# Two encoder layers unrolled: counting semaphores, a norm per token tile, projections one place forward

## What is computed

```python
def reference(x, norm_g, w_in, ..., w_branch, w_out):
    for l in range(DEPTH):                       # DEPTH = 2
        h = _rms(x, norm_g[l])
        p = jnp.einsum('bsd,de->bse', h, w_in[l])            # 1024 x 11808
        (a_qkv, a_a, a_b, a_z, b_qkv, b_z, c_q, c_k, c_v, c_z,
         d_q, d_k, d_v, d_i, d_f, d_o, d_z, gate_logits) = _split(p, PROJ_SIZES)
        y_a = _mixer_deltanet(...)   # conv of 5 taps, SiLU, gated delta rule in chunks of 64, both directions
        y_b = _mixer_natten(...)     # neighbourhood attention with a learned bias
        y_c = _mixer_gqa(...)        # grouped-query attention with axial rotary
        y_d = _mixer_mlstm(...)      # mLSTM in chunks of 64, both directions
        ys = jnp.stack([y_a, y_b, y_c, y_d], axis=2)
        proj = jnp.einsum('bsnw,nwd->bsnd', ys, w_branch[l])
        merged = jnp.sum(jax.nn.sigmoid(gate_logits...) * proj, axis=2)
        x = x + jnp.einsum('bsd,de->bse', merged, w_out[l])
```

## Time and profile before

| | us |
|---|---|
| time, median of 3 runs | 983.67 (981.82 to 983.68) |
| span of the profiled execution, first to last instruction | 982.1 |
| PE busy | 903.4 (92%) |
| DVE busy | 672.2 (68%) |
| ACT busy | 497.9 (51%) |
| POOL busy | 203.0 (21%) |
| all 464 splits on DVE (L1411) | 325.6 |
| all 464 splits on ACT (L1098) | 274.0 |

### The profile page before, as it was taken

The page is one execution under the profiler, slowest core; times in us unless marked ns, Lnnn a source line. Parts: engine busy times, 40 slices in busy tenths (PEclk is TensorE's granted clock), DMA queues, the critical chain, the costliest instruction groups (busy, mean ns, idle before and its releaser), DMA issues. The chain is left out here.

```text
span 982.1 us, 19657 instructions
## 1 busy us (share of the span) xinstructions
PE 903.4 (92%) x7206; PEld 750.8 (76%) x7206; DVE 672.2 (68%) x1209; ACT 497.9 (51%) x990; POOL 203.0 (21%) x216
## 2 busy tenths in 40 slices
PE   3998999999899999999859899999998989999996
PEld 3986778787787788778658787788877768887775
DVE  3888795667368587587459887765762776866763
ACT  3545644553454565555246555544543645564651
POOL 0301221435220014121021111222542200322210
PEclk9989999999999999999959999999999999999999
DMA  7643634424376145467156346434333832544762
GB/s 205 204 135 118 203 119 131 129 90 127 90 174 190 48 150 168 130 179 228 65 133 187 124 138 209 127 111 141 105 108 98 208 124 86 152 149 129 234 195 65
DMA packets 101403, 140.13 MB, mean 143 GB/s; under 512 B 31022, under 2 KB 45494, under 8 KB 101174
## 3 DMA queue, kind: packets, MB, share of 16 engines
q1 hardware_dynamic: 94118, 137.80, 47.4%
q10 hardware_dynamic: 7184, 1.02, 0.6%
HBM read 135.63 MB, written 7.27 MB: 146 GB/s over the span
## 5 line engine op out<-in xcount | busy, mean ns | idle before, releaser
L1411 DVE TENSOR_TENSOR w_low<-ring,w_high 128x512 fp32r<-128x512 f32 x464 | 325.6, 743 | 112.5 <-ACT w_high L1098 112.4
L1098 ACT ACTIVATE w_high<-ring 128x512 fp32r<-128x512 f32 x464 | 274.0, 627 | 87.2 <-PE pj L605 44.3
L603 PE MATMUL pj<-w_high,h_high 128*128 128x512 f32 x592 | 245.1, 414 | 8.7 <-DVE w_low L1411 7.9
L605 PE MATMUL pj<-w_high,h_low 128*128 128x512 f32 x592 | 234.2, 396 | 0.0
L604 PE MATMUL pj<-w_low,h_high 128*128 128x512 f32 x592 | 234.1, 395 | 0.0
L603 PEld LDWEIGHTS pj<-w_high,h_high 128*128 128x128 f32 x592 | 113.4, 191 | 36.4 <-DVE w_low L1411 8.3
L605 PEld LDWEIGHTS pj<-w_high,h_low 128*128 128x128 f32 x592 | 112.9, 191 | 24.8
L604 PEld LDWEIGHTS pj<-w_low,h_high 128*128 128x128 f32 x592 | 113.4, 192 | 22.5 <-issue 1.0
L1103 ACT ACTIVATE big<-pair 128x512 f32<-128x512 f32 (+2 forms) x136 | 60.9, 482 | 77.0 <-PE pair L780 37.1
L603 PE MATMUL mb<-w_high,h_high 128*128 128x512 f32 x112 | 44.4, 397 | 3.1 <-DVE h_low L1860 3.1
L1933 POOL TENSOR_TENSOR big<-big,tab 128x256 f32<-128x256 f32 x40 | 34.6, 881 | 48.6 <-ACT big L1255 25.0
(11 more groups left out here) (282 smaller groups left out, 1553.6 us busy)
## 6 DMA issues: line engine op xcount, KB each, us to landing
ring<-in_w_in SPq DMA_DIRECT2D x368, 256.0 KB, 3.2
ring<-in_w_branch SPq DMA_DIRECT2D x64, 256.0 KB, 3.0
ring<-in_w_out SPq DMA_DIRECT2D x32, 256.0 KB, 3.2
big<-skew SPq DMA_DIRECT2D x32, 128.0 KB, 3.7
skew<-lines SPq DMA_DIRECT2D x16, 224.0 KB
out_x<-btm SPq DMA_DIRECT2D x12, 256.0 KB, 3.8
btm<-out_x SPq DMA_DIRECT2D x8, 256.0 KB, 4.7
tab<-in_table SPq DMA_DIRECT2D x1, 1408.0 KB, 7.8
```

The source lines that it names most:

```text
L603: mm(o, r32(a), r32(b), start=start, stop=False, skip_group_check=True)
L605: return mm(o, r32(a_low), r32(b), start=False, stop=stop, skip_group_check=True)
L1098: f(r32(w_high[:, u % PARTS]), ring[:, u % RAW], ACT.Copy).then_inc(w_rounded, 1)
L1411: tt(r32(w_low[:, u % PARTS]), ring[:, u % RAW], w_high[:, u % PARTS], ALU.subtract).then_inc(w_split, 1)
```

## The change

Both layers are written out in one block; the loop, the barriers and the clearing of semaphores are gone. Every semaphore counts on: a wait of layer 1 adds what layer 0 has signalled. Layer 1's parameters are loaded by SP in layer 0, from unit `branch:3,0` on.

Each engine has an order of its own, taken from one common order of steps, in which splits are words (`split+4`), and several steps are in two parts. The projections stand one place forward: `za` is first, with token tile 0 ahead of tile 1; `c` stands where `za` was, `zc` where the second block of `c` was, and so on; `gate:0,1` stands ahead of `branch:0,0`, and at the end `branch:3,0` and `branch:3,1` follow each other. `merge_turn.0` stands behind `branch:3,1`. In layer 0 `out:1` computes units 2 to 7 of tile 0 and then of tile 1.

The norm is made by token tile: squares of half a row, POOL's power for one tile (with sqrt(1024) put into the eviction), one scaling that takes in the gain from a broadcast row (`g_row`), ACT's rounding and DVE's subtraction straight from PSUM. The first two units of a layer have slots of their own (`EXTRA`), in the place of `y_high` and `y_low`. SP stores the result by blocks of 512 columns, as soon as each residual is done. The bias loads of attention b stand behind `gate:0,0`.

The core of the diff (renamed waits, `x` to `*at(x)`, and moved code are left out):

```diff
-        with nc.Fori(0, DEPTH) as layer:
-            with nc.Block() as block:
+            for layer in range(DEPTH):
+                now[0] = layer
+        def at(signal, n):
+            return signal, now[0] * signals[signal.num] + n
...
             @block.sync
             def _(sp):
+                load_x(sp, 0)
+                for unit in range(2):
+                    load_unit(sp, unit)
+                load_x(sp, 1)
+                for unit in range(2, RAW):
+                    load_unit(sp, unit)
                 sp.dma_start(tab[:, P:n_const], table[:, P:n_const]).then_inc(table_in, 16)
-                sp.wait_ge(ident_in, 16)
-                sp.wait_ge(x_loaded, 64)
             @block.scalar
             def _(act):
                 act.dma_start(tab[:, 0:P], table[:, 0:P]).then_inc(ident_in, 16)
+                load_rows(act, 0)
+                load_cols(act, 0)
...
+                    if layer == 0:
+                        for n in range(PARAMS):
+                            load_param(act, 0, n)
+                    def square(t, q, of=layer):
+                        sl = slice(q * WB, (q + 1) * WB)
+                        f(xh[:, t, sl], x[:, t, sl], ACT.Square, accum_out=ssx[:, t, q:q + 1]).then_inc(x_squared, 1)
+                    def turn_h(t, q):
+                        f(r32(h_high[v]), four(bank_of(("hT", t, q)).t), ACT.Copy, scale=float(D) ** 0.5).then_inc(h_rounded, 1)
...
+                    def scale(t, of=layer):
+                        for q in range(2):
+                            sl = slice(q * WB, (q + 1) * WB)
+                            stt(xh[:, t, sl], x[:, t, sl], rsx[:, t:t + 1], g_row[:, sl], ALU.mult, ALU.mult).then_inc(h_ready, 1)
+                    def turn_h(t, q):
+                        stt(r32(h_low[v]), four(b.t), float(D) ** 0.5, h_high[v], ALU.mult, ALU.subtract).then_inc(b.free, 1)
...
-            nc.all_engine_barrier()
-            nc.sync.sem_clear(range(min(nums), max(nums) + 1))
-            nc.all_engine_barrier()
...
+                        for block_, t in ((0, 0), (0, 1), (1, 0), (1, 1)):
+                            sp.wait_ge(*released(("pj", "out", block_, t)))
```

PE's order, the places that the text speaks of (before, then after):

```diff
-    norm conv:0:0+4 conv.0 conv:1:0+4 conv.1 silu.0 gatecols conv:2:0+4 gatecols_turn conv.2 silu.1 conv:3:0+4 conv.3 silu.2 a_turn.0 rope za:0:0+2
-    za:0:2+2 silu.3 conv:4:0+4 cols conv.4 a_turn.1 a_norm silu.4 conv:5:0+4 za:0:4+2 a_scale conv.5 za:0:6+2 silu.5 a_qkt c:0:0+2 a_kkqk a_turn.2
+        turn_h.0.0 turn_h.0.1 za:0:0+4@0 turn_h.1.0 za:0:4+2@0 turn_h.1.1 za:0:6+2@0 za:0:0+2@1 taps za:0:2+4@1 za:0:6+2@1 conv:0:0+4 conv:1:0+4
+        gatecols conv:2:0+4 gatecols_turn conv:3:0+4 c:0:0+2 a_turn.0 c:0:2+2 conv:4:0+4 cols a_turn.1 conv:5:0+4 c:0:4+2 c:0:6+2 a_qkt c:1:0+2
...
-    gate:3,1:0+2 gate:3,1:2+2 gate:3,1:4+2 gate:3,1:6+2 merge_turn.0 merged.0 branch:3,1:0+2 branch:3,1:2+2 out:0:0+2 out:0:2+2 merge_turn.1 merged.1
+        gate:3,1:4+2 gate:3,1:6+2 branch:3,0:0+2 branch:3,0:2+2 branch:3,1:0+2 branch:3,1:2+2 merge_turn.0 out:0:0+2 out:0:2+2 merge_turn.1 out:0:4+2
```

DVE's order at the start of a layer after the change:

```diff
+        turn_h.0.0 turn_h.0.1 scale.1 turn_h.1.0 split+2 turn_h.1.1 split+2 take:za:0@0 taps small take:za:0@1 gain_a split+8 conv.0 split+4 conv.1
+        silu.0 split+4 gates_in gates_out conv.2 silu.1 split+4 conv.3 silu.2 split+4 silu.3 split+4 cols conv.4 a_norm.0 a_norm.1 silu.4 split+6
```

More of the change, by code:

```diff
@@ L54 @@
 WB, CUN = 512, 4
[L55 removed]
+RAW, PARTS, EXTRA = 6, 6, 2
 TILE_OF = (0, 1, 1, 0)
@@ new lines, in order @@
+def order(engine):
+    start, layer, between, end = ORDER[engine]
+    layers, split = [], 0
+    for n in range(DEPTH):
+        steps = []
+        for word in ((start if n == 0 else "") + layer + (end if n == DEPTH - 1 else between)).split():
+            if ":" in word:
+                name, arg, span = word.split(":")
+                step = name if name in ("take", "add") else "proj"
+                span, _, token = span.partition("@")
+                tokens = range(NT) if token == "" else (int(token),)
+                if step == "proj":
+                    arg = tuple(map(int, arg.split(",")))
+                    steps.append(("proj", name, arg if len(arg) > 1 else arg[0], *map(int, span.split("+")), tokens))
+                else:
+                    block = tuple(map(int, span.split(",")))
+                    steps.append((step, arg, block if len(block) > 1 else block[0], tokens[0]))
+            elif "+" in word:
+                count = int(word.split("+")[1])
+                steps.append(("split", range(split, split + count)))
+                split += count
+            else:
+                name, *args = word.split(".")
+                steps.append((name, *map(int, args)))
+        layers.append(steps)
+    return layers
@@ L166, in weight_plan @@
+def weight_plan(layers):
     first = {"conv": A_QKV, "za": A_Z, "c": C_QKV, "zc": C_Z, "b": B_QKV, "zb": B_Z, "d": D_QKV, "o": D_O, "zd": D_Z, "out": 0}
     plan = []
[L168 to L178, removed]
@@ L179, in weight_plan @@
-    return plan
+    for layer, stages in enumerate(layers):
+        for name, *args in stages:
+            if name != "proj" or args[4] == (1,):
+                continue
+            kind, arg, u, n = args[:4]
+            if kind == "branch":
+                col = arg[1] * WB
+            elif kind == "gate":
+                col = GATES + arg[0] * D + arg[1] * WB
+            else:
+                col = first[kind] + arg * (CW if kind == "conv" else WB)
+            plan += [(layer, kind, arg, u + i, col) for i in range(n)]
@@ new lines, in run, with released_before, load_unit @@
+        def run(engine, **steps):
+            for name, *args in orders[engine][now[0]]:
+                steps[name](*args)
+        dve_count, pool_count = [0], [0]
+        before = {}
+        def released_before(key):
+            bank, n, _ = before[key]
+            return bank.free, n
+        def load_unit(sp, unit):
+            layer, kind, arg, u, col = plan[unit]
+            if unit >= RAW:
+                sp.wait_ge(w_split, unit - RAW + 1)
+            if kind == "conv":
+                src = w_in[layer, u * CK * P:(u + 1) * CK * P, col:col + CW].rearrange("(k p) n -> p k n", p=P)
+                dst = ring[:, unit % RAW].rearrange("p (k n) -> p k n", k=CK)
+            else:
+                src = w_branch[layer, arg[0]] if kind == "branch" else (w_out if kind == "out" else w_in)[layer]
+                src, dst = src[u * P:(u + 1) * P, col:col + WB], ring[:, unit % RAW]
+            sp.dma_start(dst, src).then_inc(ring_full[unit % RAW], 16)
```

990 lines of the change are left out of this document (508 added, 482 removed).

## The result

The changed kernel takes 1008.40 us, median of 4 runs (1004.53 to 1011.43), against 982.75 (980.55 to 983.68) for the kernel before: 1.0259 times as long, 95% interval 1.0230 to 1.0288. It is slower by 26 us where 13 us less were forecast. The profiled execution has a span of 1009.4 us, against 982.1.

A forecast was written before the change was run, and what follows sets the result against it. PE's work bounds the kernel, plus its waits and half-clock spells: -16.8 - 2.0 - 2.8 - 1.2 + 1.4 + 1.6 + 4.6 + 1.7 = -13.5, giving 968.6, or 970.2 us as median; range 949 to 979.

The forecast's parts named there:

- Boundary, -16.8: Between the layers: without loop and barriers, with tile 0's norm covered by products, the 20.0 us seam becomes 3.2.
- Start, -2.0: Before the first product: ACT free at about 9.1 us after 15 DMAs, first product at about 16.8; saves 2.0 us.
- End, -2.8: Behind the last product: no block barrier and two half-size stores behind the last residual; saves 2.8 us, between 1.3 and 3.5.
- Projections one place forward, -1.2: Convolution stage: same order on DVE, taps faster, first wait longer, one za gate wait gone; saves 1.2 us in all.
- costed at nothing: per-engine order lists with the same steps and the same waits: Whole kernel: order lists, running counters, SP's layer 1 loads and later bias loads cost nothing, hidden by the gate products.
- The convolution stage's two waits: PE's waits for SiLU output and split weights, 5.6 and 7.9 us over both layers, stay because DVE is the bound.
- the rival of dissolved waits: Convolution stage: the shifted filler removes PE's waits and half-clock spells, 20.3 us, giving 950.4 us; chance 0.18.
- POOL against DVE: za stage: 7.1 us of POOL's rope work costs DVE some 3.2 us, hidden at 17.4 against a cover of 18.2.
- the full lock: Rival, za stage: POOL's rope holds DVE for all 7.1 us, conv.0 3.1 late in both layers, 976.4 us; chance 0.08.
- z blocks, +1.4, and c_qkt, +1.6: zc and zb run straight into the next block, +1.4 us; c_qkt's rotation waits behind zc's gates, +1.6 us.
- The slower rival: At zc and zb, both layers, DVE reaches the gate behind a whole earlier step: 23.2 us, 993.4 us; chance 0.05.
- Tail, +4.6 and +1.7: Before out:0: merge_turn.0's rounding uncovered, a wait of 2.3 us a layer, +4.6, and one half-clock spell, +1.7.

The follow-up runs named there:

- x8: Kernel with the edits of x1, x2 and x3 together, but out:1 of layer 0 computed for both token tiles unit by unit: 977.22 us, ratio 0.9962.
- x1: Changed kernel with nine splits per layer moved earlier in ACT's and DVE's lists in the za stage: 985.96 us, ratio 1.0045 to the kernel before.
- after: The changed kernel itself, without follow-up edits: 1008.40 us, 1.0259 times the kernel before.
- x6: x1 with, in both layers, splits of c:0 and of c:0:4 and on moved ahead in the convolution stage: 984.27 us, ratio 1.0025.
- x9: Changed kernel with edits of x1, x2, x3, x6, merge_turn.1 one unit earlier, SP's ten parameter loads one by one behind units 8 to 17: 969.75 us.
- x3: Changed kernel with merge_turn.0 one unit ahead of the end of branch:3,1, merged.0 ahead of its evictions on DVE: 1006.00 us, ratio 1.0257.
- x4: Changed kernel with ACT's two column loads of layer 0 put last, behind the ten parameter loads: 1008.39 us, one run.
- x10: Changed kernel with layer 0's two column loads given out by SP behind the table, the rest left on ACT: 997.66 us, ratio 1.0163.
- x2: Changed kernel with layer 0's ten parameter loads given out by SP behind the table instead of by ACT: 1001.04 us, ratio 1.0171.

## Why the prediction was wrong

The forecast had 970.2 us and a range of 949 to 979; 1008.4 is outside it, on the other side of the kernel before. By its own steps:

- **Boundary, -16.8:** right in mechanism and size, with some luck in the terms. The seam of 18.25 us with 2.0 of half clock behind it became 2.82 us with the products at full pace behind it: -17.4. The forecast had 3.2 for it: 2.1 for sixteen transposes and 1.1 for PE's wait between transposes and product. The wait is 1.19, but only the eight transposes of token tile 0 lie in the seam, 1.32 us, and 0.31 pass from the last product's start to them; tile 1's eight lie inside layer 1. x8 confirms the part with the cover: 3.4 us.
- **Start, -2.0:** wrong by 9.3 us, since it was +7.3. The step that failed is "so ACT is free at about 0.7 + 15 x 0.56 = 9.1 us" (the row behind it gives 0.59 each and 9.6, which is not what matters): ACT was free at 19.8. Thirteen of the DMAs cost what was forecast, 0.54 on average; two took 8.70 and 2.95. The price came from a row in which the column loads went out at 9.71 with nothing ahead of them in ACT's queue; even there the DMA behind them took 1.44 us, three times its neighbours (0.34 to 0.47; timeline of ACT's sequencer, kernel before):

```profile
10.90 1.44 ACTq L1377 DMA_DIRECT2D small<-in_dn_norm_g  x1
```

  The forecast's bound of 2 lost allowed for DMAs slower than now, but no row was named for it, and this one was not asked why it stood out.
- **End, -2.8:** -4.1 measured; the mechanism held, but the size lies outside the forecast's 1.3 to 3.5.
- **Projections one place forward, -1.2, and "costed at nothing: per-engine order lists with the same steps and the same waits":** this is where the prediction broke. It counted the work of DVE ahead of conv.0 (17.4 us against a cover of 18.2) and found it hidden. The sum of work was not the question. za by token tiles holds all eight units of weights until tile 1 is done, two in the extra slots and six in the slots of `w_high`, and the lists put the splits for what comes next behind the transposes and behind za's last eviction. So the order of the waits was not the same, although the steps were, and DVE and ACT, with enough time in sum, stood idle for steps that PE was yet to do. Price: waits of 2.10 + 2.01 + 3.49 + 2.41 + 2.01 + 3.49 = 15.5 us and spells of 1.58 + 1.71 + 2.83 + 1.53 + 1.71 = 9.4 (PE's busy time times one minus the granted clock, summed over windows of 1 us): 24.9. x1 gave back 22.4 by the medians and 27.6 by the spans (the profiled execution of after was the slowest of its four runs, that of x1 among the faster half of its eight). The diff in front of the prediction had it in plain words: `turn_h.1.0 split+2 turn_h.1.1 split+2 take:za:0@0 ... take:za:0@1 gain_a split+8`. It can be found without a run: at each PE word, one asks for the last split that it needs and for what stands ahead of that split on ACT and on DVE.
- **The convolution stage's two waits:** stayed, as forecast. They were 5.6 + 7.9 = 13.5 and are 2 x (2.96 + 3.95) = 13.8, and the first changed its name from SiLU to `c:0`'s split. That DVE is the bound there is borne out by x6 for the stretch up to 81.87; the rival of dissolved waits (950.4) falls. The taps of conv.0 did get back to full speed (six took 2.46 in place of 3.91), which gave PE nothing that shows.
- **POOL against DVE:** the full lock (976.4) did not come, and neither did the 3.2 us of the forecast. In after DVE mostly stood idle beside the rope work (28.39 to 33.19), so it had little to lose there. In x1 two splits that lie beside POOL's rope copies take 1.32 us; alone they take 1.28. Timelines of DVE and of POOL in x1:

```profile
28.28 1.32 DVE L1563 TENSOR_TENSOR w_low<-ring,w_high 128x512 fp32r<-128x512 f32 x2
...
28.17 2.19 POOL L2102 COPY mid<-mid 128x64 f32<-128x64 f32 x4
```

  The rule of the Trainium skill (SBUF — State Buffer, "Who interferes with whom") that the loser of the shared ports is fully blocked is not borne out by this row. For the taps the loss is there and partial, as in the earlier trace rows: in x9, where the rope products fall beside conv.0 again, two TENSOR_SCALAR take 1.55 us in place of 0.61 and the six taps 3.40 in place of 2.46, 1.9 us beside 3.40 us of POOL.
- **z blocks, +1.4, and c_qkt, +1.6:** +0.4 (waits on a gate 1.1 against 0.7) and +1.2 (4.4 against 3.2). The slower rival had its place here and its price was 23.2 us; the direction came out as it said, but by another mechanism, so it explains nothing.
- **Tail, +4.6 and +1.7:** the waits are 2 x 2.31 = 4.6, as worked out; both were followed by a spell, not one, so +3.4. x3 takes them down to 0.24.

The measured terms add up to -17.4 + 7.3 - 4.1 + 24.9 + 0.3 + 0.4 + 1.2 + 4.6 + 3.4 = 20.6 of the 27.3 us. Some 3.7 more are transposes and the taps' turn, which lay ahead of the first product before and lie inside the layers now; the other 3 I have not traced.

Of the forecast's own signs the first product failed (27.59, not 16 to 18), and the others of "right" held: no gap over 2 us at the seam, 4.4 us behind the last product, waits of 2.96 and 3.95 before `c:0:0` and `c:0:4`, 2.31 before `out:0`. None of the signs of "wrong" came, and none looked at the za stage, where most of the time was lost.

## What to carry to other kernels

When steps are reordered by hand, follow every word of the consumer back: which slot and which split does it need last, and what stands ahead of that in the producer's list. A sum of work that fits says nothing when the producer waits for the consumer in between; idle time ahead of the late step (as on ACT and DVE here) tells an error of order, which a move of a few words cures (x1), from a bound, which it doesn't (x6). And a DMA issue is to be priced by what is waiting in its queue, not by the mean of its neighbours: keep loads of many small pieces away from an engine whose arithmetic is due next.

## What the runs showed of the hardware

- An engine that issued a DMA into a queue with the column loads' 2048 small pieces was held for 8.70 us in one issue and 2.95 in the next (after), 9.21 in two (x4), 7.52 in two on SP (x10); with little ahead of them the same two loads took 1.20 (x2). The Trainium skill (DMA: Bandwidth & Descriptors, "Issuing engines are not separate DMA queues") says that issuing from several engines only saves the sequencer's time, "which is usually small". Here that time was not small: moving ten issues off ACT brought the first product forward by 10.5 us.
- Waits of PE of 2.0 to 2.5 us were often followed by a spell at 1.2 GHz that costs up to 1.7 us, not always. Of the eight such waits in after five were: 2.10, 2.01, 2.41 in the za stages and 2.31 before `out:0` in both layers. Three were not: the 2.01 of layer 1, and 2.23 and 2.20 before `c_qkt`; in x6 the wait before `c_qkt` of layer 0, 2.18, was (clock 0.66 in the window 150 to 155, against 1.00 in 163 to 169 in after). The spread between runs doesn't follow the number of such waits: 6.9 us over four runs of after, but 9.5 over eight of x1, which has fewer of them.
- POOL and DVE at once: a split (two inputs, 512 columns) lost 0.02 to 0.04 us beside POOL's copies (two took 1.32 in x1, three 2.00 in x9, against 1.28 and 1.89 alone), the taps of conv.0 took 3.40 against 2.46 beside POOL's products (x9).
